# Diagonal seams, grouped modulation, fox weights scaled on VectorE, weight parts ahead of filter steps, and one more step for head norms in a four-layer kernel

## What is computed

```
first block, l = 0, 1:
  h = rms_norm(x, g[0])
  mix = concat(hgrn2_mix(...), rglru_mix(...)) @ even_w_out     # l = 0
  mix = fox_attention(q, k, v, f) @ odd_w_out                   # l = 1
  x = x + rms_norm(mix, g[1])
  x = x + rms_norm(conv_ffn(rms_norm(x, g[2]), ...), g[3])      # d_ff 2816, conv over 3 tokens
fox_attention: logits = q k + c_q - c_k, causal; p = softmax(logits); o = p v
second block, l = 0, 1:
  shift, scale, gate = split(silu(cond) @ w_mod[l] + b_mod[l])
  h = rms_norm(x, g) * (1 + scale) + shift                      # for lat and for ctx
  l = 0: hyena (short conv, long conv by a filter made by an MLP and divided by
         the sum of its magnitudes) and attention (8 heads, 2 key heads, q and k
         normalised per head, rotary on lat), both gated, @ w_out
  l = 1: mLSTM over chunks, forward and backward, gated, normed per head, @ w_out
```

## Time and profile before

| | |
|---|---|
| median of 3 runs | 1766.73 us (1765.39 to 1773.41) |
| profiled execution | 1768.96 us, its span 1765.8 us |
| mean granted TensorE clock | 0.968 |
| busy share PE / PE weight load | 91% / 76% |
| busy share DVE / ACT / POOL | 62% / 47% / 8% |
| moved by DMA | 217.73 MB, mean 123 GB/s |

### The profile page before, as it was taken

The page is one execution under the profiler, slowest core; times in us unless marked ns, Lnnn a source line. Parts: engine busy times, 40 slices in busy tenths (PEclk is TensorE's granted clock), DMA queues, the critical chain, the costliest instruction groups (busy, mean ns, idle before and its releaser), DMA issues.

```text
span 1765.8 us, 24010 instructions
## 1 busy us (share of the span) xinstructions
PE 1615.4 (91%) x9364; PEld 1349.3 (76%) x9364; DVE 1099.0 (62%) x2040; ACT 837.4 (47%) x1529; POOL 147.0 (8%) x163
## 2 busy tenths in 40 slices
PE   7976999979979998979999899999997979999998
PEld 6865899968858877857768676787776768888876
DVE  6666667775558868665465777615546565464665
ACT  5845544555656555442204454332325335455564
POOL 1100000121310203010000000000001001000000
PEclk9998999999989999989999999999998989999999
DMA  6423666634326544524401111124422212342323
GB/s 241 154 96 119 219 234 219 202 129 144 120 90 203 173 134 122 165 84 167 162 6 60 59 37 48 61 71 167 156 95 84 84 60 95 96 133 82 132 101 126
DMA packets 61888, 217.73 MB, mean 123 GB/s; under 512 B 7888, under 2 KB 8144, under 8 KB 61648
## 3 DMA queue, kind: packets, MB, share of 16 engines
q1 hardware_dynamic: 58608, 212.40, 35.9%
q10 hardware_dynamic: 3168, 3.80, 0.7%
HBM read 215.09 MB, written 1.05 MB: 122 GB/s over the span
## 4 chain that ended last, share of the span: by engine, by line
PE 63%; DVE 14%; ACT 12%; issue 7%; POOL 2%; ACTq 1%; DMA 0%; DVEq 0%; POOLq 0%
PE PS L328 18%; PE PS L329 17%; PE PS L330 17%; DVE WL L304 4%; ACT WH L293 3%; PE PS L2525 2%; PE PS L1954 2%; PE PS L1963 2%; PE PS L749 1%; POOL AR L465 1%; ACT TMP L396 1%; POOL AR L1506 1%; PE PS L758 1%; PE PS L2556 1%; DVE RB L512 1%
## 5 line engine op out<-in xcount | busy, mean ns | idle before, releaser
L304 DVE TENSOR_TENSOR WL<-RAWB,WH 128x1024 fp32r<-128x1024 f32 x346 | 434.4, 1263 | 239.2 <-ACT WH L293 236.0
L328 PE MATMUL PS<-RH,WH 128*128 128x256 f32 (+1 forms) x1560 | 506.2, 325 | 26.0 <-DVE WL L304 12.3
L329 PE MATMUL PS<-RH,WH 128*128 128x256 f32 (+1 forms) x1560 | 495.0, 317 | 0.0
L330 PE MATMUL PS<-RH,WL 128*128 128x256 f32 (+1 forms) x1560 | 494.2, 317 | 0.0
L293 ACT CAST WH<-RAWB 128x1024 fp32r<-128x1024 f32 x346 | 357.3, 1041 | 235.1 <-PE PS L330 190.6
L328 PEld LDWEIGHTS PS<-RH,WH 128*128 128x128 f32 x1560 | 302.6, 194 | 54.9 <-ACT RH L493 7.2
L328 PE MATMUL PS<-WH,RH 128*128 128x512 f32 (+1 forms) x768 | 309.2, 403 | 21.1 <-DVE WL L304 12.7
L329 PEld LDWEIGHTS PS<-RH,WH 128*128 128x128 f32 x1560 | 302.8, 194 | 18.2 <-issue 0.5
L330 PEld LDWEIGHTS PS<-RH,WL 128*128 128x128 f32 x1560 | 302.2, 194 | 18.5
L329 PE MATMUL PS<-WL,RH 128*128 128x512 f32 (+1 forms) x768 | 299.5, 390 | 0.0
L330 PE MATMUL PS<-WH,RH 128*128 128x512 f32 (+1 forms) x768 | 299.2, 390 | 0.0
(11 more groups left out here) (339 smaller groups left out, 1718.2 us busy)
## 6 DMA issues: line engine op xcount, KB each, us to landing
RAWB<-ws SPq DMA_DIRECT2D x394, 512.0 KB, 3.6
TMP<-gains ACTq DMA_DIRECT2D x8, 256.0 KB, 2.9
CS<-cs SPq DMA_DIRECT2D x1, 1472.0 KB, 10.3
X<-x SPq DMA_DIRECT2D x2, 512.0 KB, 4.0
X<-ctx SPq DMA_DIRECT2D x2, 512.0 KB, 6.8
AR<-dec ACTq DMA_DIRECT2D x2, 512.0 KB, 7.2
out<-X SPq DMA_DIRECT2D x4, 256.0 KB, 2.0
AR<-rgw SPq DMA_DIRECT2D x1, 512.0 KB, 4.4
```

The costliest lines, as they stand in the source:

```text
L304: dve.e.tensor_tensor(k.WL[:, i % SPL, :], k.RAWB[:, i % RAW, :], k.WH[:, i % SPL, :].bitcast(F32), ALU.subtract).then_inc(*dve.done("wl", i))
L328: pe.e.matmul(o, wh, xh, start=first, stop=False)
L329: pe.e.matmul(o, wh, xl, start=False, stop=False)
L330: return pe.e.matmul(o, wl, xh, start=False, stop=last)
```

## The change

- **Seams.** `scale` and `scale_act` go. VectorE writes one 128x128 diagonal of a block's roots (`diagonal_dve`), and TensorE multiplies the residual X itself by that diagonal (`turn_pe` is a matmul and not a transpose), which turns and scales at once. The mean over the first half and the epsilon are taken in before the second half's sum (`mean_dve`), the second half comes in through the logarithm's bias and scale (`root_act`); the correction is one instruction shorter (`root_dve`). The order in `seam_act` and `seam_dve` changes: means stand before the gained products, ScalarE's sums of the first block before the output's last ones, and `rest_to` behind both diagonals.
- **Modulation.** Four units make a group: a product is 256 columns wide and there are 4 to a unit; the bank is held for four units, and the copy, the turn and the bias come once per group. `ffn_mod` gains a step for the last turn; the four last units use the same functions. `c_sum4` has four columns.
- **fox.** The scaling by the reciprocal moves from GpSimd behind the reciprocal on VectorE.
- **ffn1 (and ffn0).** `out_ahead` (the casts and low parts for the output product) comes ahead of the filter's and the ctx norm's steps on VectorE and ScalarE; ScalarE's filter step moves behind the step's own split, GpSimd's behind its gating; the filter's reciprocal goes in two halves over two steps.
- **Attention.** k and q units have four steps, of which the third is empty: the rotary turn is a round later.

```diff
-        self.c_sum4 = self.CS[:, a + 4:a + 6]
+        self.c_sum4 = self.CS[:, a + 4:a + 8]
...
-    for h in range(2):
-        dve.wait_ge(*k.ACT.at(s, kind, tb, "ss", h))
-    dve.e.tensor_scalar(v, c0, c1, 1.0 / 1024, ALU.add, ALU.mult).then_inc(*dve.done(s, kind, tb, "v"))
+    dve.wait_ge(*k.ACT.at(s, kind, tb, "ss", 0))
+    dve.e.tensor_scalar(v, c0, 1.0 / 1024, EPS, ALU.mult, ALU.add).then_inc(*dve.done(s, kind, tb, "v"))
     dve.wait_ge(*dve.last())
-    dve.e.tensor_scalar(w, v, EPS, None, ALU.add).then_inc(*dve.done(s, kind, tb, "w"))
+    dve.e.tensor_scalar(w, v, -0.5, None, ALU.mult).then_inc(*dve.done())
 
 
 def root_act(k, act, s, kind, tb):
 
     c0, c1, v, r, w = stat(k, s, kind, tb)
-    act.wait_ge(k.s_cs, 16)
     act.wait_ge(*k.DVE.at(s, kind, tb, "v"))
-    act.e.activation(r, v, ACT.Ln, bias=k.c_eps, scale=1.0).then_inc(*act.done())
+    act.wait_ge(*k.ACT.at(s, kind, tb, "ss", 1))
+    act.e.activation(r, c1, ACT.Ln, bias=v, scale=1.0 / 1024).then_inc(*act.done())
     act.wait_ge(*act.last())
     act.e.activation(r, r, ACT.Exp, scale=-0.5).then_inc(*act.done(s, kind, tb, "r0"))
 
...
 def root_dve(k, dve, s, kind, tb):
 
     c0, c1, v, r, w = stat(k, s, kind, tb)
-    dve.wait_ge(*k.DVE.at(s, kind, tb, "w"))
+    dve.wait_ge(*k.ACT.at(s, kind, tb, "ss", 1))
+    dve.wait_ge(*dve.last())
+    dve.e.scalar_tensor_tensor(w, c1, -0.5 / 1024, w, ALU.mult, ALU.add).then_inc(*dve.done())
+    dve.wait_ge(*dve.last())
     dve.wait_ge(*k.ACT.at(s, kind, tb, "r0"))
-    dve.e.tensor_scalar(c0, w, r, r, ALU.mult, ALU.mult).then_inc(*dve.done())
+    dve.e.tensor_scalar(w, w, r, r, ALU.mult, ALU.mult).then_inc(*dve.done())
     dve.wait_ge(*dve.last())
-    dve.e.tensor_scalar(c0, c0, -0.5, 1.5, ALU.mult, ALU.add).then_inc(*dve.done())
-    dve.wait_ge(*dve.last())
-    dve.e.tensor_tensor(r, r, c0, ALU.mult).then_inc(*dve.done(s, kind, tb, "r"))
+    dve.e.scalar_tensor_tensor(r, w, 1.5, r, ALU.add, ALU.mult).then_inc(*dve.done(s, kind, tb, "r"))
...
-def scale_act(k, act, s, tb, h, turned):
-
-    act.wait_ge(*k.DVE.at(s, "p", tb, "r"))
-    act.e.activation(turned[:, half(h)], k.X[:, tb, half(h)], ACT.Identity, scale=stat(k, s, "p", tb)[3]).then_inc(
-        *act.done(s, "y", tb, h))
-
-
-def scale(k, eng, s, tb, h, turned):
-
-    eng.wait_ge(*k.DVE.at(s, "p", tb, "r"))
-    eng.e.tensor_scalar(turned[:, half(h)], k.X[:, tb, half(h)], stat(k, s, "p", tb)[3], None, ALU.mult).then_inc(
-        *eng.done(s, "y", tb, h))
-
-
-def turn_pe(k, pe, s, q, i, n, turned, take=True):
+def diagonal_dve(k, dve, s, tb, dg):
+
+    dve.wait_ge(k.s_cs, 16)
+    dve.wait_ge(*k.DVE.at(s, "p", tb, "r"))
+    dve.e.tensor_scalar(dg, k.ident, stat(k, s, "p", tb)[3], None, ALU.mult).then_inc(*dve.done(s, "diag", "p", tb))
+
+
+def turn_pe(k, pe, s, q, i, n, dg, take=True):
+
 
     b = k.ps.take(pe, s, "turned", q, i) if take else k.ps.of(s, "turned", q, i)
-    pe.wait_ge(k.s_cs, 16)
-    for who in (k.ACT, k.DVE, k.POOL):
-        pe.wait_ge(*who.at(s, "y", 2 * q + n, i // 2))
+    pe.wait_ge(*k.DVE.at(s, "diag", "p", 2 * q + n))
     for j in range(2):
         c = 128 * (2 * i + j)
-        t = pe.e.transpose(b[:, 256 * j + 128 * n:256 * j + 128 * n + 128], turned[:, c:c + 128], k.ident)
+        t = pe.e.matmul(b[:, 256 * j + 128 * n:256 * j + 128 * n + 128], k.X[:, 2 * q + n, c:c + 128], dg, start=True, stop=True)
     t.then_inc(*pe.done(s, "turned", q, i, n))
...
         put_out(second, 0)
+        if m.t:
+            taken_in(first, 0)
         put_out(second, 1)
         root_act(k, act, m.s, "o", second)
-    if m.t:
+        if m.t:
+            taken_in(first, 1)
+            root_act(k, act, m.t, "p", first)
+            cast_to(k, act, m.opens(k))
+    else:
         taken_in(first, 0)
         taken_in(first, 1)
-        if m.s:
-            cast_to(k, act, m.opens(k))
+        root_act(k, act, m.t, "p", first)
+    if m.t:
         taken_in(second, 0)
-        root_act(k, act, m.t, "p", first)
         taken_in(second, 1)
         root_act(k, act, m.t, "p", second)
         if not m.s:
             cast_to(k, act, m.opens(k))
-        scale_act(k, act, m.t, second, 0, m.turned[1])
...
     if m.s:
         dve.wait_ge(k.s_gain, 32 * gain)
+        mean_dve(k, dve, m.s, "o", first)
         gained(first, 0)
         gained(first, 1)
-        root(m.s, "o", first)
+        root_dve(k, dve, m.s, "o", first)
         residual_dve(k, dve, m.s, first, 0)
         residual_dve(k, dve, m.s, first, 1)
+        mean_dve(k, dve, m.s, "o", second)
         gained(second, 0)
-        mean_dve(k, dve, m.s, "o", second)
+        if m.t:
+            mean_dve(k, dve, m.t, "p", first)
         gained(second, 1)
         root_dve(k, dve, m.s, "o", second)
         residual_dve(k, dve, m.s, second, 0)
         residual_dve(k, dve, m.s, second, 1)
     if m.t:
-        mean_dve(k, dve, m.t, "p", first)
-        if m.s:
-            rest_to(k, dve, m.opens(k))
+        if not m.s:
+            mean_dve(k, dve, m.t, "p", first)
         root_dve(k, dve, m.t, "p", first)
-        root(m.t, "p", second)
-        scale(k, dve, m.t, second, 1, m.turned[1])
-        if not m.s:
-            rest_to(k, dve, m.opens(k))
+        diagonal_dve(k, dve, m.t, first, m.diag[0])
+        mean_dve(k, dve, m.t, "p", second)
+        root_dve(k, dve, m.t, "p", second)
+        diagonal_dve(k, dve, m.t, second, m.diag[1])
+        rest_to(k, dve, m.opens(k))
...
-    for h in range(2):
-        scale(k, pool, m.t, 2 * m.q, h, m.turned[0])
...
-    b = k.ps.take(pe, "mod", u)
+
+    g, n = divmod(u, 4)
+    l, c = divmod(4 * g, 24)
+    b = k.ps.hold(pe, "mod", g) if n == 0 else k.ps.of("mod", g)
     pe.wait_ge(*k.DVE.at("silu"))
-    for i in range(8):
-        w, end = weights(k, pe, False, f"w_mod{l}", i, c)
-        g = 32 * (i % 4)
-        mm = pe.e.matmul(b[g:g + 32, 0:128], k.SCC[:, 2 * i:2 * i + 32], w, start=i < 4, stop=i > 3)
+    for i in (2 * n, 2 * n + 1):
+        for h in range(2):
+            w, end = weights(k, pe, False, f"w_mod{l}", i, c + 2 * h, 2)
+            r = 32 * (2 * (i % 2) + h)
+            mm = pe.e.matmul(b[r:r + 32, 0:256], k.SCC[:, 2 * i:2 * i + 32], w, start=n == 0, stop=n == 3)
     mm.then_inc(*pe.done("weights", end))
-    pe.mark("mod", u)
-
-
-def mod_turn_pe(k, pe, u):
+    if n == 3:
+        pe.mark("mod", g)
+
+
+def mod_turn_pe(k, pe, g):
 
     pe.wait_ge(k.s_cs, 16)
-    pe.wait_ge(*k.DVE.at("modrow", u))
-    pe.e.matmul(k.ps.of("mod", u)[:, 256:258], k.modrow[u > 15].of(u), k.c_sum4, start=True, stop=True).then_inc(*pe.done("modt", u))
-    k.modrow[u > 15].free(pe, u)
-
-
-def mod_row_dve(k, dve, u):
-    row = k.modrow[u > 15].take(dve, u)
-    dve.wait_ge(*k.PE.at("mod", u))
-    dve.e.tensor_copy(row, k.ps.of("mod", u)[:, 0:128]).then_inc(*dve.done("modrow", u))
-
-
-def mod_turn_dve(k, dve, u):
...
-    return j - 1 if l == 0 and 1 <= j <= 16 else None
+    return j - 1 if l == 0 and 1 <= j <= 17 else None
...
+        u = ffn_mod(l, j)
+        if u == 16:
+            mod_turn_pe(k, pe, 3)
+        elif u is not None:
+            mod_unit_pe(k, pe, u, u == 0)
...
-            if ffn_filter(l, j) is not None:
-                filter_act(k, act, *FILTER_STEPS[ffn_filter(l, j)])
+            if j >= FFN_LAG:
+                out_ahead(k, act, s, [j - FFN_LAG], cast_to)
...
+            if ffn_filter(l, j + 2) is not None:
+                filter_act(k, act, *FILTER_STEPS[ffn_filter(l, j + 2)])
...
+            if j >= FFN_LAG:
+                out_ahead(k, dve, s, [j - FFN_LAG], rest_to)
             if ffn_filter(l, j) is not None:
                 filter_dve(k, dve, *FILTER_STEPS[ffn_filter(l, j)])
             if ffn_ctx(l, j) == -1:
...
+            if ffn_filter(l, j + 1) is not None:
+                filter_pool(k, pool, *FILTER_STEPS[ffn_filter(l, j + 1)])
...
-                pe.wait_ge(*k.POOL.at(s, "p", h, i))
+                pe.wait_ge(*k.DVE.at(s, "p", h, i))
...
+                x = L.PP.of(s, "p", h, qb)[:, 0:128 * (qb + 1)]
                 dve.wait_ge(*k.ACT.at(s, "exp", h, qb))
-                v.reciprocal(rs, su).then_inc(*dve.done(s, "inverse", h, qb))
+                v.reciprocal(rs, su).then_inc(*dve.done())
+                dve.wait_ge(*dve.last())
+                v.tensor_scalar(x, x, rs, None, ALU.mult).then_inc(*dve.done(s, "p", h, qb))
...
-ATT_STEPS = [(*ATT_UNITS[u], p) for u, p in rounds([{"k": 3, "q": 3, "v": 1, "a": 3, "g": 1}[n] for n, _ in ATT_UNITS])]
+
+ATT_STEPS = [(*ATT_UNITS[u], p) for u, p in rounds([{"k": 4, "q": 4, "v": 1, "a": 3, "g": 1}[n] for n, _ in ATT_UNITS])
+             if ATT_UNITS[u][0] in "avg" or p != 2]
...
-    elif p == 2:
+    elif p in (2, 3):
+        cc = slice(256 * (p - 2), 256 * (p - 2) + 256)
         dve.wait_ge(*k.PE.at(s, "norm", c))
         dve.wait_ge(*k.DVE.at(s, "hf", c - 1, 3))
-        v.reciprocal(L.NI, k.ps.of(s, "norm", c)).then_inc(*dve.done(s, "norm", c))
```

(7 more changed lines are left out.)

175 lines of the change are left out of this document (70 added, 105 removed).

## The result

The changed kernel takes 1755.16 us (median of 4 runs, 1753.99 to 1756.17) where the kernel before takes 1768.79 (median of 4, 1765.39 to 1773.41): a ratio of 0.9921, 95% interval 0.9895 to 0.9947, thus 14 us less, where 32.5 were forecast. The profiled execution has a span of 1752.3 us.

The account below looks back on a forecast made before the run. TensorE, busy 1615.4 of 1765.8 us, was taken as the bound, with its waits and the lower clock behind them. Five terms, 8.0 + 5.0 + 5.5 + 8.0 + 6.0 = 32.5 us, gave a median of 1734, range 1721 to 1750.

Parts of the forecast that it names:

- part 3: Fox attention: softmax scaling moved from GpSimd to VectorE ends TensorE's ten waits; 5.5 us less, bounds 2.5 and 7.5.
- part 4: Second feed-forward block: weight parts put ahead of filter steps end waits for low parts; 8.0 us less, bounds 3 and 12.
- part 5: Second block's attention: rotary turn a round later ends TensorE's waits for it; 6.0 us less, bounds 2 and 9.
- Part 1: Seams: TensorE turns and scales by a diagonal in place of GpSimd's scaling; 8.0 us less, bounds 0 and 13.
- Part 2: Feed-forward modulation in groups of four units, with fewer turning products; 5.0 us less, bounds 3 and 7.
- the slower rival: Modulation: products of 256 columns run one behind another, 54 us more, thus 1788 us; chance 0.04.
- the filter gets late: Second feed-forward block: sums of magnitudes come after TensorE asks, two new waits of 2 to 4 us; 1742 us, chance 0.06.
- the reciprocal is halved: Second feed-forward block's filter: splitting VectorE's reciprocal of 3.36 us helps low weight parts come earlier; no separate size given.
- the softmax weights are the next to be late: Second block's attention: new waits of about 1.9 us after each of two long pieces, 3.8 us taken off the gain.
- The 3.4 us for the clock: Second block's attention: gain from ending the lower clock behind two of the waits for the rotary turn.
- The vector chains take over: Seams and attention: VectorE and ScalarE chains bind next, so gains there halve; 17 us less, 1750 us, chance 0.20.
- Products bring the clock up sooner: Six seams: products count as activity where transpositions don't, so the full clock comes earlier; 5.6 us, 1728 us, chance 0.08.

## Why the prediction was wrong, point by point

Three of the five terms failed, 19.5 of the 32.5 us. In part 3 waits of TensorE were taken for time on the path, in part 4 the moved and halved filter steps were costed at nothing in the sum, and in part 5 the costs of the extra step were undersized and its gain from the clock was taken as certain.

- **Part 1: right, with a term that was booked elsewhere.** Forecast 8.0, measured alone 9.7 (6.9 to 12.6), of which the traces put 10.5 in the seams, 5.0 in the second feed-forward block and -7.8 in the stages between. The seam before fox went by its steps: the turn starts 4.75 us after the last output product where 7.59 stood, 2.84 earlier (forecast 2.7), and 32 products take until 376.30 (6.1 us, forecast 6.8 less 0.7). In the opening seam the turn starts 2.2 us earlier (7.26 for 9.43) and 32 products take 5.3 us, where 16 transpositions with their hole took 5.5; their spacing falls from 0.213 to 0.112 us after 14 of them in this trace, after 18 to 28 in four others, and the seam gains 1.0 to 2.5 us (forecast 0.6). The products cost twice the transpositions, two instructions of 0.112 us for one of 0.11, as the rows had it. So the trace stays with the row against the ratio of four in the Trainium skill (page TensorE: Matmul & The Clock Gate, section Terms).
- **Part 2: right.** Forecast 5.0 with bounds 3 and 7, measured 3.9. 8 instructions of 256 columns take 0.64 us, as 16 of 128 did; the slower rival, that column groups stop overlapping, fell.
- **Part 3: the step from "TensorE's ten waits of up to 0.7 us sum to 5.8" to 5.5 us less time failed.** The size was right, 5.1 measured, but only where ScalarE's issues are gone; as made it is 0.8 in the stage. The step took a wait of the busiest engine for time on the path. The rows of the waits could not show it; the pace of the loop could: 9.60 us, exactly repeated, while TensorE's wait in it could shrink. I followed who released TensorE, and not who released the releaser: the maximum on VectorE, ScalarE, its issues. ScalarE's queue, with its four issues, had not been looked at. The 8 us of work for VectorE are 10.3: a scaling of 256 columns takes 0.355 us there, one of 128 takes 0.286, where the row of 0.294 was of another line.
- **Part 4: the waits went as forecast, and two replaced them.** The rival *the filter gets late* named the first, with 0.06 and 8 us, on the margin that "TensorE reads them a step (8.7 us) later, against the 8 to 9 us that I count for the chain": a margin of nothing, taken as cover. The second was not among my steps: "the reciprocal is halved" was costed as a gain, and its bank, which the second half holds for a step more, was not followed, though four of the eight banks are taken by the output and the rest turn over in each step. Together 10.9 us; without them the stage gains 11.2 (235.0 to 223.8), of which 5.0 come with part 1.
- **Part 5: the two costs were named and both undersized.** The first score product waits 2.6 us, not 1.3, for the 1.22 us of a weight part ahead of the rotation were left out; behind it the clock is at 0.50 in this trace, 1.6 us more. The second, "the softmax weights are the next to be late", comes at four waits of 1.1 to 2.9 us and not at two of 1.9, and at the steady pairs the turn product had been free filling of a wait. The 3.4 us for the clock didn't come: where two old waits were followed by the lower clock, two new ones are. Against it stand the 1.1 us of the wait of 1.42, which were not forecast. The stage gains 0.5 us in this trace and 3.7 in the four whose clock stays up, where 6.0 were forecast.
- **Rivals.** *The vector chains take over* (1750, 0.20) is nearest in time, with 1755.16 in its span of 1744 to 1757, and in kind, but its story was one of degree; what happened are four separate places. *Products bring the clock up sooner*: no: outside the opening seam the spacing falls in this trace after 22 to 28 products, 4.8 to 6.1 us behind the start, about as after the transpositions of before.

The spectrum's -1.8 us are the clock too. In every trace TensorE waits 2.5 to 2.9 us for the copy of the modulation's last row there (L758 in the changed kernel). From the last projection of the short convolutions to the attention's first the kernel before takes 62.7 us and the two kernels in which GpSimd issues the transfers 62.9, all three with the full clock behind that wait; nine kernels take 64.5, the changed one among them with 0.51, and one 65.5, with a longer stretch at 0.50. The changed kernel, first row, and the one with GpSimd issuing, second row:

```profile
873.80:876.80 3.00, 3.00 (x14) 2.68 (x13) 0.00 (x0) 2.21 (x4) 0.00 (x0) 0.51 0.04 15
866.60:869.60 3.00, 3.00 (x17) 2.02 (x16) 0.00 (x0) 2.06 (x4) 0.00 (x0) 1.00 0.05 21
```

What stays open: why the clock falls behind a wait in one execution and not in another. And part 4's gain apart from its two new waits was not run alone: 11.2 us without them, less the 5.0 that come with part 1, is a difference of traces.
